# Sparse attention on one core: value products taken key block by key block, the transposed weights of a branch kept whole

## The reference

```python
o_c = einsum('bgrqn,bgnd->bgrqd', p_c, v_cmp)      # 31 compressed keys
o_s = einsum('bgrqk,bgqkd->bgrqd', p_s, v_sel)     # selected blocks
o_w = einsum('bgrqk,bgkd->bgrqd', p_w, v_w)        # window of 512
return g[..., 0:1] * o_c + g[..., 1:2] * o_s + g[..., 2:3] * o_w
```

## Time and profile before

| | us |
|---|---|
| median of 3 runs | 2016.63 (2013.88 to 2021.2) |
| the profiled execution, its own time | 2024.83 |
| its span, from the first instruction to the last | 2023.1 |
| TensorE busy with matmuls | 1776.0 (88%) |
| VectorE busy | 735.6 (36%) |
| ScalarE busy | 416.4 (21%) |
| mean granted clock of TensorE | 0.946 |

### The profile page before, as it was taken

One profiled execution on the slowest core, in us unless ns is written; L12 is line 12 of the kernel. 1 busy time (PEld: TensorE's weight loads), 2 busy tenths in 40 slices (PEclk: granted clock), 3 DMA queues, 4 the chain that ended last, 5 costly groups with the idle time before them and its releaser, 6 DMA issues. The chain is left out here.

```text
span 2023.1 us, 21863 instructions
## 1 busy us (share of the span) xinstructions
PE 1776.0 (88%) x8048; PEld 982.2 (49%) x8048; DVE 735.6 (36%) x1856; ACT 416.4 (21%) x1044; POOL 102.4 (5%) x126
## 2 busy tenths in 40 slices
PE   4999996988998999998978778788799999898787
PEld 2656553445666888656333233232354455533232
DVE  5344445563556644363111111111412554321114
ACT  3223222203443000012111011010300330231111
POOL 1100000000000000000000000000000000011100
PEclk8999997989999999998999999998889999798989
DMA  9532335761120622544999999999111234499994
GB/s 377 190 142 105 116 122 194 266 252 50 40 79 12 253 100 85 230 171 194 427 426 428 426 427 427 426 429 396 71 52 57 85 144 161 181 422 425 423 413 166
DMA packets 67909, 474.84 MB, mean 235 GB/s; under 512 B 11311, under 2 KB 12527, under 8 KB 42976
## 3 DMA queue, kind: packets, MB, share of 16 engines
q1 hardware_dynamic: 51200, 399.12, 48.7%
q0 software_dynamic: 15456, 70.22, 9.1%
q10 hardware_dynamic: 1152, 4.19, 0.5%
HBM read 459.99 MB, written 33.59 MB: 244 GB/s over the span
## 5 line engine op out<-in xcount | busy, mean ns | idle before, releaser
L2102 PE MATMUL moe_ps<-moe_up,moe_hg 128*64 128x512 f32 x1536 | 381.3, 654 | 106.6 <-DMA moe_up<-in_exp_gate 41.2
L2102 PEld LDWEIGHTS moe_ps<-moe_up,moe_hg 128*64 128x64 f32 x1536 | 133.1, 150 | 351.4 <-issue 351.0
L491 PE MATMUL hg_proj<-hT,hg_w 128*128 128x512 f32 x384 | 171.3, 603 | 6.5 <-DMA hg_w<-in_w_hg 6.5
L2139 PE MATMUL moe_ps<-moe_down,moe_midT 128*64 128x512 f32 x720 | 161.1, 596 | 11.8 <-DMA moe_down<-in_exp_down 10.5
L2192 ACT ACTIVATE moe_sig<-moe_ps 128x512 f32<-128x512 f32 (+1 forms) x32 | 15.7, 492 | 544.5 <-PE moe_ps L2102 544.5
L2221 DVE COPY moe_midT<-moe_ps 128x512 f32<-128x512 f32 (+1 forms) x32 | 17.9, 558 | 283.7 <-PE moe_ps L2111 283.7
L491 PEld LDWEIGHTS hg_proj<-hT,hg_w 128*128 128x128 f32 x384 | 72.6, 192 | 95.3 <-issue 87.0
L2231 DVE SCALAR_TENSOR_TENSOR moe_res<-moe_ps,moe_route_slot_share,moe_gain 128x512 f32<-128x512 f32 x64 | 45.1, 747 | 157.0 <-PE moe_ps L2139 157.0
L2139 PEld LDWEIGHTS moe_ps<-moe_down,moe_midT 128*64 128x64 f32 x720 | 52.9, 137 | 99.3 <-issue 96.3
L2177 ACT ACTIVATE moe_hg<-moe_ps,mod,scale_ffn 128x128 f32<-128x128 f32 x248 | 90.2, 468 | 48.7 <-PE moe_ps L2085 48.7
L2653 PE MATMUL p_ps<-hT,p_w 128*128 128x512 f32 x192 | 87.4, 619 | 2.4 <-PEq L2521 2.4
(11 more groups left out here) (382 smaller groups left out, 2466.2 us busy)
## 6 DMA issues: line engine op xcount, KB each, us to landing
moe_down<-in_exp_down SPq DMA_DIRECT2D x45, 2048.0 KB, 28.9
moe_up<-in_exp_up SPq DMA_DIRECT2D x32, 2048.0 KB, 29.1
moe_up<-in_exp_gate SPq DMA_DIRECT2D x32, 2048.0 KB, 29.3
moe_up<-in_exp_in SPq DMA_DIRECT2D x32, 2048.0 KB, 32.8
rest_w<-in_mod_rest POOLq DMA_DIRECT2D x16, 1536.0 KB, 7.8
hg_w<-in_w_hg SPq DMA_DIRECT2D x32, 512.0 KB, 3.5
rest_w<-in_mod_rest POOLq DMA_DIRECT2D x8, 2048.0 KB, 8.5
xn<-in_w_merge SPq DMA_DIRECT2D x32, 512.0 KB, 4.7
```

The lines of the kernel that those rows point to most:

```text
L491: last = pe.matmul(proj[bank][:, :], w[s][:, kc, :], k.hT[:, kc, :], start=(kc == 0), stop=(kc == KC - 1))
L2102: last = pe.matmul(self.up_ps[u][e * SLOTS:(e + 1) * SLOTS, :], self.hg[m % 2][:, kc, e * SLOTS:(e + 1) * SLOTS], w[:, kc, :], start=(kc = ...
L2139: last = pe.matmul(self.res_ps[side][e * SLOTS:(e + 1) * SLOTS, :], self.midT[:, f, e * SLOTS:(e + 1) * SLOTS], w[e][:, f, side * 512:(sid ...
```

## The change

The transposed weights of both branches are kept whole: `at_pT` is two tiles of 4 x 512 columns instead of two of 512, one for each branch. ScalarE's copy puts the blocks of unit c, one key block each, 512 columns apart at its query block. The mix of a branch is no longer done unit by unit but once, key block by key block: key block kk meets all queries from its own block on, 512, 384, 256 and 128 columns. A head has three mixes instead of nine, and `mixed` counts so. In TensorE's order branch 0 is mixed in step 5 of its head, branch 1 in step 0 of the next head and the compressed branch in step 1 of it, each behind the projection's part. The output is kept one unit later.

```diff
-        pT = [k.sb(ctx, f"at_pT{s}", [P, SEQ]) for s in range(2)]
+        pT = [k.sb(ctx, f"at_pT{br}", [P, TC, SEQ]) for br in range(2)]
...
-                def mix(h, s, u):
-                    pe.wait_ge(S["pT_ready"], h * NU + (u + 1))
-                    if u == 0:
+                def mix(h, s, br):
+
+
+                    pe.wait_ge(S["pT_ready"], h * NU + (min(TC * (br + 1), NU)))
+                    if br == 0:
                         pe.wait_ge(S["values_ready"], stagings(h, s))
                         if not isinstance(h, int) or h >= 2:
                             pe.wait_ge(S["o_kept"], h - 1)
-                    if u < len(UNITS):
-                        br, c = UNITS[u]
-                        for kk in range(c + 1):
-                            last = pe.matmul(o_ps[s][:, c * P:(c + 1) * P], values[:, br, kk, :], pT[u % 2][:, kk * P:(kk + 1) * P],
-                                             start=(u == 0), stop=False, skip_group_check=True)
+                    if br < 2:
+                        for kk in range(TC):
+                            last = pe.matmul(o_ps[s][:, kk * P:SEQ], values[:, br, kk, :], pT[br][:, kk, kk * P:SEQ],
+                                             start=(br == 0 and kk == 0), stop=False, skip_group_check=True)
...
-                        if u:
-                            mix(h, s, u - 1)
-                        elif after_first(h):
-                            mix(h - 1, 1 - s, NU - 1)
+                        if u == 5:
+                            mix(h, s, 0)
+                        elif u < 2 and after_first(h):
+                            mix(h - 1, 1 - s, u + 1)
...
-                mix(HEADS - 1, 1, NU - 1)
+                mix(HEADS - 1, 1, 1)
+                mix(HEADS - 1, 1, 2)
...
-                        if u >= 2 or after_first(h):
-
-                            act.wait_ge(S["mixed"], h * NU + (u - 1))
-                        n = (UNITS[u][1] + 1) * P
-                        act.activation(pT[u % 2][:, 0:n], tr[u % 2][:, 0:n], ACT.Copy).then_inc(S["pT_ready"], 1)
+                        br, c = UNITS[u]
+                        if c == 0 and after_first(h):
+                            act.wait_ge(S["mixed"], h * 3 + (br - 2))
+                        act.activation(pT[br][:, 0:c + 1, c * P:(c + 1) * P], tr[u % 2][:, 0:(c + 1) * P].rearrange("p (k n) -> p k n", n=P),
+                                       ACT.Copy).then_inc(S["pT_ready"], 1)
...
-                            act.wait_ge(S["mixed"], h * NU)
+                            act.wait_ge(S["mixed"], h * 3)
...
-                    dve.wait_ge(S["mixed"], h * NU + NU)
+                    dve.wait_ge(S["mixed"], h * 3 + 3)
...
-                        if u == 2 and after_first(h):
+                        if u == 3 and after_first(h):
                             keep_output(h - 1, 1 - s)
...
-                        pool.wait_ge(S["mixed"], h * NU)
+                        pool.wait_ge(S["mixed"], h * 3)
```

## The result

The changed kernel takes 2033.9 us at the median of 15 executions, the one before 2020.6 us at the median of its 15. The ratio is 1.0073, with a 95% interval of 1.0055 to 1.0091: slower by 14.7 us (11 to 18). Slower was forecast, but with 8.7 us; the loss is larger than that by more than its interval. (The time itself, 2033.9, is 8.5 us above the forecast 2025.4; 4.0 of these are that the kernel before has its median at 2020.6 here and had 2016.6 in the three runs that the forecast started from.)

What follows compares the result with a forecast made beforehand. TensorE was taken to bound the attention stage, with about 8 us of gaps. Head 0 at -0.8, heads 1 to 6 at +7.5 and the last head at +2.0 gave +8.7 us on 2016.6: 2025.4, range 2017 to 2034.

Steps and rivals of the forecast that it cites:

- its own signs of being wrong: A head under 21.4 us, no wait before turn(5), stage clock below 1.00, or a later stage giving the time back.
- the stalls: TensorE waits before unit 5's transposes (0.6 us), and before unit 8's and the next head's first, together 0.7 us more.
- head 0: First head, with no mixes of a head before it: 19.6 us against 20.43, -0.8 us.
- heads 1 to 6: Six heads of 22.60 us against 21.31, plus 0.3: 135.9 us against 128.4, +7.5 us.
- last head: No projection: unit 8's transposes 0.7 us later (bounds 0 and 1.3), then 1.27 more of mix; +2.0 us.
- The clock falls: Rival: TensorE's busy share drops to 88%, the stage's clock to 0.93, costing 12 us, total 2037; 6 in 100.
- 4.66 us from turn(6): Head's end, unit 6's transposes to the next head's first: 0.76 + 2.12 + 1.78 us, with some 2.5 of TensorE work.
- 1.78 for turn(8) to turn(0): Unit 8's transposes to the next head's first, waiting for ScalarE's copy of the compressed weights: 1.78 us.
- 0.3 us for the loop: Allowance within heads 1 to 6 for the slightly longer heads inside the loop: 0.3 us.
- The long mix as cover: Rival: branch 0's 2.16 us mix lets VectorE get ahead; heads of 19.9 us, total about 2006; 7 in 100.
- One stall only: Rival: one of the two stalls (0.6 and 0.7 us) is missing; 4 us less, 2021; 27 in 100.
- The slower copy: ScalarE's copy into pieces a row apart: between 0 and 0.5 us more a head, 4 us in all; taken as zero.

Runs made afterwards that it cites:

- experiments 4 and 9: Changed kernel plus unread TensorE products filling the gaps in steps 7 and 8; ratio 1.0043 to the kernel before, stage 173.2 us in both profiles.
- experiment 6: Changed kernel with branch 1 mixed in step 8 of its own head and the compressed branch in step 0 of the next; ratio 1.0018 to the kernel before.
- experiment 11: Changed kernel with an unread 512-column product filling step 7 alone; stage 173.2 us in one profile.
- experiments 6 to 8: Branch 1 mixed in step 8, 1.0018; then with ScalarE's copies swapped and branch 0's mix spread, 0.9985; then unswapped, compressed mix in step 4, 0.9966.
- experiments 3 and 7: Changed kernel with branch 0's mix spread over steps 5 to 8, 1.0009; spread over steps 5 to 7, branch 1 in step 8, ScalarE's copies swapped, 0.9985.
- experiment 2: Changed kernel, swapped on ScalarE: copy of unit 3 ahead of the next head's queries; ratio 1.0025 to the kernel before, stage 168.9 us, 175.2 when profiled again.
- experiment 1: Kernel before, its order and mixes kept, with only the whole-tile storage and strided ScalarE copy; ratio 1.0001, stage 163.5 us.
- experiment 12: Changed kernel with key blocks in pieces of 128 columns, 20 passes a branch; a mix takes 2.23 us instead of 2.16, one profile.

## Why the prediction was right in kind and too small in size

Its account of the order was right, and the stalls stand where it put them; one of its own signs of being wrong came true, a granted clock below 1.00 in the stage. The stage lost 13.2 us where the sum had 8.7. The terms that were too small miss by 5.1 us; that the last head was taken 0.7 too long, and hides part of this, is luck. Term by term, with the filled kernel of experiments 4 and 9 as the one without falls:

| term | forecast | measured |
|---|---|---|
| head 0 | -0.8 | -0.7 (19.69 against 20.43) |
| heads 1 to 6 | +7.5 | +9.2 (137.6 against 128.4) |
| last head | +2.0 | +1.3 (15.88 against 14.59, to the last compressed mix) |
| falls of the clock | 0, a rival with 6 in 100 | +3.4 (176.6 against 173.2) |
| sum | +8.7 | +13.2 |

*The step that failed.* "The clock falls" was set apart as a rival that does the whole thing or nothing, at 12 us and 6 in 100. It was argued from mean busy shares: 88% was near the last head's 89%, which had 1.00. The runs show a third way. The falls come in some heads, each costing 1.4 to 1.7 us: two in each profile of the changed kernel, none and four in those of the swapped one, one (in the last head) in that of the pieces, none in three profiles of the filled ones. Filling leaves the heads as long as they are without a fall. So the term that the sum had at nothing is worth 3.4 us.

The timed executions bear on the cause more broadly than the few profiles. Their granted clock, as a mean over the whole kernel, is 0.9438 for the changed kernel (21 executions) and 0.9442 for the swapped one (12), but 0.9460 for the filled one (12) and 0.9459 and 0.9462 for the kernel before (35 and 29); the standard error of each is at most 0.0008. The other five kernels lie between 0.9456 and 0.9479, so the two with both gaps and no filling are the lowest of all. The missing 0.0022 is some 9 us of 2030 at half speed, by this estimate 2 or 3 falls of 3.4 us an execution, if the other stages are alike in all. That the gaps bring the falls is well supported, not proven. Which combination it takes is less sure: experiment 6 kept the gap before turn(8) and lost the one before turn(0), experiment 11 the other way round, and neither had a fall, each in one profile; what decides in a given head is open. The times agree: the filled kernel is at 1.0043, where the stage's +9.8 us would be 1.0048, and the changed one at 1.0073 and 1.0085, whose intervals both hold the 1.0065 of +13.2 us.

*Heads 1 to 6* were taken at 22.60 us and are 22.94 on average. The 4.66 us from turn(6) had 1.78 for turn(8) to turn(0), and that is what heads 0 and 6 show; it was read from the start of the copy, without what the copy itself waits for. The others take 1.99, 1.83, 2.33, 1.84 and 1.92. What is more comes from VectorE, through the chain of logits, exponential and copy shown above. From the start of its last work on unit 8 (L1260) to its next logits it takes 0.21 us in the heads that are written out, 0.41 on entering the loop, 0.25 inside, 0.75 on going round from head 3 to head 4 (566.59 - 565.84) and 0.33 on leaving; in the kernel before it is the same to 0.01. In that kernel the mix behind turn(8) covered it, up to the longest: turn(8) to turn(0) was 2.00 everywhere but at that one, 2.33. I had added 0.3 us for the loop; it took 1.0 at this place. Another 1.0 over the six heads stands before turn(8), which comes at 20.89 to 21.13 us of a head instead of 20.82, latest in heads 2 and 4, as before the change (19.49 against 19.2 to 19.3). In experiments 6 to 8, with a mix behind turn(8) again, turn(8) to turn(0) is 3.26 or 3.27 in every head.

*The last head's* turn(8) came at 13.26 us of the head, as before (13.24). VectorE took up all of the 1.3 us, the lower of the two bounds, and the 1.27 us of the mix behind it remained.

*The rivals.* The long mix as cover fell by experiments 3 and 7: it gives VectorE time where it has enough, and takes it at the next head's scores. One stall only: both are there, and experiment 2 prices the first at 4.3 us. The slower copy is zero, as taken (experiment 1). What kept the waits short before was the spread of the mixes: those in steps 4 to 8 stood where TensorE would have waited for another engine. The products are the same to 1 us (experiment 12).

## What to carry to other kernels

On an in-order engine that runs a pipeline by hand, work that nobody waits for is cover. Joining nine small pieces into three large ones saved 1 us of issue here and uncovered some 11 us of waits (7.4 to 18.9 by the rows, 9.8 net in the stage); the same key blocks, split and moved to where the engine would wait, gained 6. So before moving a piece, list for each step what the engine will wait for next, and put the piece just ahead of that wait and behind whatever another engine needs early. Here gaps of 0.5 to 1.3 us cost more than themselves, as TensorE's clock fell behind some of them, and that part of the loss differed from run to run.

## What the runs showed that I had not expected

- The granted clock fell to 1.2 GHz behind stretches where TensorE was never idle for more than 1.3 us at a time (busy 3.68 of the 5.5 us ahead of a fall), in zero to four heads of the same program, and was back 3.4 us later. With useless products in the gaps no fall is seen in three profiles, and the mean clock of 12 executions is that of the kernel before.
- At the edges of VectorE's loop 0.12 to 0.54 us passed between two of its instructions beyond the 0.21 in heads that are written out (0.41 on entering, 0.75 on going round, 0.33 on leaving, 0.25 inside). In the changed kernel TensorE paid them (1.99, 2.33, 1.92 and 1.83 us from turn(8) to turn(0) against 1.78); with a mix of 2.16 us behind turn(8) it paid nothing.
- ScalarE wrote four pieces 512 columns apart in the same 583 ns as one contiguous piece.
